# Two transformer blocks on one core: loads of the first stage reordered, a 16-row series cut in three, one weight unit of the scan rounds moved into the chain of steps

## The reference

```
mod = silu(c) @ w_ada + b_ada                    # 12288 numbers for each block
shift_m, scale_m, gate_m, shift_f, scale_f, gate_f = split(mod, 6)
h = rms_norm(x, g) * (1 + scale_m) + shift_m
proj = h @ w_in        ->  q, k, v, xs, z, B, C, dt_raw
dt = softplus(dt_raw + dt_bias)                  # 16 heads x 256 tokens, first block
A_cs = cumsum(dt * -exp(a_log))
x = x + gate_m * mix ;  h = ... ;  x = x + gate_f * conv_ffn(h)
```

## Time and profile before

| what | value |
| --- | --- |
| median of 3 runs | 2723.0 us (2719.33 to 2724.44) |
| the profiled execution, its own time | 2718.6 us |
| its span, first to last instruction | 2716.7 us |
| PE busy | 2491.7 us, 92% of the span |
| DVE busy | 1883.8 us, 69% |
| ACT busy | 1114.1 us, 41% |
| mean granted TensorE clock | 0.951 |
| read from HBM | 607.54 MB |

### The profile page before, as it was taken

One profiled execution on the slowest core, in us unless ns is written; L12 is line 12 of the kernel. 1 busy time (PEld: TensorE's weight loads), 2 busy tenths in 40 slices (PEclk: granted clock), 3 DMA queues, 4 the chain that ended last, 5 costly groups with the idle time before them and its releaser, 6 DMA issues.

```text
span 2716.7 us, 51420 instructions
## 1 busy us (share of the span) xinstructions
PE 2491.7 (92%) x21636; PEld 2411.4 (89%) x21636; DVE 1883.8 (69%) x2215; ACT 1114.1 (41%) x1179; POOL 87.8 (3%) x184
## 2 busy tenths in 40 slices
PE   4889885989999999999979999899899999999997
PEld 4888854989999999999969888789899999999997
DVE  5988768877777677776769766667777654555544
ACT  3234323345554334443343445333555433344433
POOL 0000000000000000000000000000000000000000
PEclk9999966999999999999989999899899999999999
DMA  7987723957776887777938422216576545455442
GB/s 318 392 337 278 283 115 134 367 219 278 278 287 242 332 287 275 277 278 282 329 138 325 159 85 85 99 64 235 213 270 243 184 171 185 170 186 178 177 171 108
DMA packets 87914, 613.56 MB, mean 226 GB/s; under 512 B 9576, under 2 KB 13168, under 8 KB 14320
## 3 DMA queue, kind: packets, MB, share of 16 engines
q1 hardware_dynamic: 64608, 442.95, 44.6%
q0 software_dynamic: 23184, 168.83, 16.1%
HBM read 607.54 MB, written 4.21 MB: 225 GB/s over the span
## 4 chain that ended last, share of the span: by engine, by line
PE 81%; DVE 12%; ACT 3%; issue 2%; DMA 1%; SPq 0%; DVEq 0%; ACTq 0%
PE ps L686 24%; PE ps L688 24%; PE ps L687 24%; DVE first_raw L1484 2%; PE ps L683 2%; DVE w_lo L1472 2%; ACT w_hi L1011 1%; DMA tri<-in_consts 1%; PE ps L573 1%; DVE w_lo L1468 1%; PE ps L818 1%; DVE rstd L1503 1%; PE ps L467 1%; DVE tmp L1511 1%; DVE xbc L1616 1%
## 5 line engine op out<-in xcount | busy, mean ns | idle before, releaser
L686 PE MATMUL ps<-h_hi,w_hi 128*128 128x256 f32 x4480 | 1288.3, 288 | 78.9 <-DVE h_lo L1597 28.3
L688 PE MATMUL ps<-h_hi,w_lo 128*128 128x256 f32 x4480 | 1278.6, 285 | 0.0
L687 PE MATMUL ps<-h_lo,w_hi 128*128 128x256 f32 x4480 | 1278.5, 285 | 0.0
L1468 DVE TENSOR_TENSOR w_lo<-w_raw,w_hi 128x2048 fp32r<-128x2048 f32 x307 | 703.7, 2292 | 534.8 <-ACT w_hi L1006 531.0
L1006 ACT CAST w_hi<-w_raw 128x2048 fp32r<-128x2048 f32 x306 | 583.5, 1907 | 1005.2 <-PE ps L688 972.2
L686 PEld LDWEIGHTS ps<-h_hi,w_hi 128*128 128x128 f32 x4480 | 871.2, 194 | 90.2 <-issue 33.6
L687 PEld LDWEIGHTS ps<-h_lo,w_hi 128*128 128x128 f32 x4480 | 871.6, 195 | 0.4
L688 PEld LDWEIGHTS ps<-h_hi,w_lo 128*128 128x128 f32 x4480 | 870.4, 194 | 0.0
L686 PE MATMUL ps<-hid_hi,w_hi 128*128 (+1 forms) x1408 | 397.3, 282 | 21.8 <-issue 21.8
L687 PE MATMUL ps<-hid_lo,w_hi 128*128 (+1 forms) x1408 | 396.6, 282 | 0.0
L688 PE MATMUL ps<-hid_hi,w_lo 128*128 (+1 forms) x1408 | 396.4, 282 | 0.0
(11 more groups left out here) (331 smaller groups left out, 1531.8 us busy)
## 6 DMA issues: line engine op xcount, KB each, us to landing
w_raw<-in_w_stream SPq DMA_DIRECT2D x376, 1024.0 KB, 4.8
ada_raw<-in_ada_stream POOLq DMA_DIRECT2D x160, 1024.0 KB, 6.8
first_raw<-in_ada_stream SPq DMA_DIRECT2D x32, 1024.0 KB, 7.4
x<-in_x_t SPq DMA_DIRECT2D x1, 2048.0 KB, 13.8
x_kept<-x SPq DMA_DIRECT2D x1, 2048.0 KB, 7.3
out_t<-x SPq DMA_DIRECT2D x4, 512.0 KB, 2.7
ada_c<-in_c SPq DMA_DIRECT2D x1, 1024.0 KB, 4.4
ada_c<-in_c POOLq DMA_DIRECT2D x1, 1024.0 KB, 6.1
```

The costliest lines, as they stand in the source:

```text
L686: mm(o, hi, r_hi, start=first, stop=False, **kw)
L687: mm(o, hi, r_lo, start=False, stop=False, **kw)
L688: return mm(o, lo, r_hi, start=False, stop=last, **kw)
L1468: tt(w_lo[:, slot], w_raw[:, slot], w_hi[:, slot % 2].bitcast(F32), ALU.subtract).then_inc(lo_ready, 1)
```

## The change

1. **Loads and order of the first stage.** SP issues c, ones, x, params, rows 0 to 3, weight unit 0, rows 4 to 7; then for k = 1 to 15 weight unit k followed by rows 2(k + 3) and 2(k + 3) + 1 as long as k + 3 < 16; ident, tri and rel_bias behind all of these. DVE makes eight products ahead of the variance, and products within the loop from k = 4 on. `stat(0)` waits for ones alone; the wait for the other two constants goes to the first transpose that needs them. ACT takes the root ahead of the casts of units 0 and 1.
2. **Softplus in three parts** (5, 8 and 6 statements) behind units (5, 3), (6, 0) and (6, 3). The products of (5, 3) and (6, 3) are taken out, one is put at (6, 2), and five instead of four stand ahead of `var(3)`.
3. **Sixth unit of the rounds**: two of its eight parts behind the `u` product of each of the four steps, in rounds 0, 1 and 3.

```diff
             sp.dma_start(ada_c[:], a["c"].partition_broadcast(P)).then_inc(c_in, 16)
-            sp.dma_start(par[:], a["params"]).then_inc(par_in, 16)
-            load_first_ada(0)
-            load_first_ada(1)
             sp.dma_start(ones[:], a["consts"][:, CCOL["ones"]:CCOL["ones"] + P]).then_inc(con_in, 16)
             sp.dma_start(x[:], a["x_t"]).then_inc(x_in, 16)
-            load_first_ada(2)
-            load_first_ada(3)
+            sp.dma_start(par[:], a["params"]).then_inc(par_in, 16)
+            for q in range(4):
+                load_first_ada(q)
             load_w(U_QK, 0, True)
-            load_w(U_QK + 1, 1, True)
+            for q in range(4, 2 * AHEAD):          # AHEAD = 4
+                load_first_ada(q)
+            for k in range(1, KT):
+                load_w(U_QK + k, k % 4, k < 4)
+                if k + AHEAD - 1 < KT:
+                    load_first_ada(2 * (k + AHEAD - 1))
+                    load_first_ada(2 * (k + AHEAD - 1) + 1)
             sp.dma_start(ident[:], ...)
             sp.dma_start(tri[:], ...)
             sp.dma_start(relb[:], a["rel_bias"]).then_inc(relb_in, 16)
-            for k in range(2, KT):
-                load_first_ada(2 * k)
-                load_first_ada(2 * k + 1)
-                load_w(U_QK + k, k % 4, k < 4)
             units(KT, U_OUT1 + 4)
...
                     last.then_inc(S("u_mm"), 1)
+                if i != 2:
+                    pair(*units[5], ks=(2 * q, 2 * q + 2))
                 if q == 3:
                     break
...
-            if i != 2:
-                pair(*units[5], ks=(0, 2))      # ahead of y_sum
...
-            if i != 2:
-                pair(*units[5], ks=(2, 4))      # behind y_sum
...
-            if i != 2:
-                pair(*units[5], ks=(4, 8))      # behind y_sq_sum
...
-            pe.wait_ge(con_in, 48)
+            pe.wait_ge(con_in, 16)
             stat(0)
...
             pe.wait_ge(S("decays"), 1)
+            pe.wait_ge(con_in, 48)
...
             stat(0, xs, 0)
+            root(0)
             hi_unit(U_QK)
             hi_unit(U_QK + 1)
-            root(0)
...
-            for q in range(4):
+            for q in range(2 * AHEAD):
                 first_ada(q)
             var(0, D)
             inverse(0)
             for k in range(KT):
-                if k >= 2:
+                if k >= AHEAD:
                     first_ada(2 * k)
                     first_ada(2 * k + 1)
...
-            in1_ada = (..., (1, 1, 1, 1), (0, 1, 0, 1), (1, 1, 1, 1))
+            SOFTPLUS = {(5, 3): 0, (6, 0): 1, (6, 3): 2}
+            in1_ada = (..., (1, 1, 1, 0), (0, 1, 1, 0), (1, 1, 1, 1))
...
                     next_ada(in1_ada[c][i])
-                if c == 6:
-                    softplus()
+                    if (c, i) in SOFTPLUS:
+                        softplus(SOFTPLUS[c, i])
...
-            next_ada(4)
+            next_ada(5)
```

More of the change, by code:

```diff
@@ L43 @@
 FFN_A, FFN_B = 12, 10
+AHEAD = 4
 UNIT = 2048
@@ L1629, in in1_evac, with softplus @@
                     V.tensor_copy(v_tok[:, 1, o:o + 512], ps[:, 4 * par_ + 1, :]).then_inc(dve_evac, 1)
-            def softplus():
+            def softplus(part):
                 XV, EV, SV, S2 = (sp_w[:, i] for i in range(4))
                 NA = sp_w[:, 4, 0:1]
[L1635 to L1648, removed]
@@ new lines, in softplus @@
+                if part == 0:
+                    dve.wait_ge(S("dt_exp"), 2)
+                    steps.link(ts(SV, EV, 2.0, None, ALU.add))
+                    steps.link(V.reciprocal(SV, SV))
+                    steps.link(tt(SV, SV, EV, ALU.mult))
+                    steps.link(tt(S2, SV, SV, ALU.mult))
+                    steps.link(ts(EV, S2, 1.0 / 19.0, None, ALU.mult))
+                elif part == 1:
+                    for k in range(8, 0, -1):
+                        steps.link(stt(out=EV, in0=EV, scalar=1.0 / (2 * k + 1), in1=S2, op0=ALU.add, op1=ALU.mult))
+                else:
+                    steps.link(stt(out=EV, in0=EV, scalar=1.0, in1=SV, op0=ALU.add, op1=ALU.mult))
+                    steps.link(ts(XV, XV, 0.0, None, ALU.max))
+                    steps.link(stt(out=dtcs[:, 0], in0=EV, scalar=2.0, in1=XV, op0=ALU.mult, op1=ALU.add))
+                    steps.link(ts(SV, dtcs[:, 0], NA, -1.0, ALU.mult, ALU.mult))
+                    steps.link(V.memset(S2, 1.0))
+                    V.tensor_tensor_scan(dtcs[:, 1], S2, SV, 0.0, ALU.mult, ALU.add).then_inc(S("decays"), 1)
@@ L1656, in next_ada @@
                     pair += 1
-            in1_ada = ((0, 0, 0, 1), (1, 1, 1, 1), (0, 1, 1, 1), (0, 1, 1, 1), (0, 1, 1, 1), (1, 1, 1, 1), (0, 1, 0, 1),
+            SOFTPLUS = {(5, 3): 0, (6, 0): 1, (6, 3): 2}
+            in1_ada = ((0, 0, 0, 1), (1, 1, 1, 1), (0, 1, 1, 1), (0, 1, 1, 1), (0, 1, 1, 1), (1, 1, 1, 0), (0, 1, 1, 0),
                        (1, 1, 1, 1))
```

## The result

| | before | after |
| --- | --- | --- |
| median (runs) | 2721.16 us (4, 2719.03 to 2724.44) | 2803.53 us (4, 2798.23 to 2810.57) |
| ratio, 95% interval | | 1.0303 (1.0275 to 1.0332) |
| profiled execution, span | 2716.7 us | 2798.3 us |
| mean granted clock | 0.951 | 0.940 |

The change costs 82.4 us; the forecast was +84.4 us and 2807 us. Most lines of the kernel after stand three or four lower: L1481 is the product (L1484 before), L1469 the lower part, L1008 the cast and L1594 `h_lo` of the first stage, L682 to L684 PE's three products.

What follows compares the result with a forecast made beforehand. TensorE was busy 92% of the span, with DVE bounding the first stage at 7.87 us a turn. Terms +92.6 - 7.5 + 4.3 - 5.0 = +84.4 us on 2723.0 gave 2807 us, range 2790 to 2832.

Steps and rivals of the forecast that it cites:

- The ring of the first stage: First stage: each weight unit issued behind its own turn's products, a closed chain; ten turns of 17.7 us, +92.6 us.
- t(4): First stage: end of the second DVE product of turn 4, forecast at 65.9 against 72.0 before, 6.1 us ahead.
- the term of issue and landing: First stage: time from a turn's second product until its weight unit has been issued and has landed, taken as 8.7 us.
- either bound: First-stage landing limits: 7.9 us gives 16.9 a turn, +85 (chance 0.13); 10.8 gives 19.8, +114 (0.07).
- The 7.5 us: Softplus: PE's wait for a lower part behind the uncut series, forecast to vanish once cut, -7.5 us.
- The fifth product: Ahead of the attention's var(3): its load goes only once the third product is done, delaying the variance, +4.3 us.
- Rounds 0 and 1 end 2.2 us sooner: Scan rounds: full products in the steps keep the clock at 2.4 GHz, so these two rounds each end 2.2 us sooner.
- Nothing is won by the exchange itself: Rounds' tail: moving the pieces into the steps leaves 16.4 us against 16.3; only the clock changes.
- Round 3 is bound by its tail, and wins 0.6: Last scan round: bound by cast, lower part and add_half(5), so it gains only 0.6 us.
- the rounds lose: Rival, scan rounds: clock stays low in spite of the added parts, +15 us for the three, 2827 us; chance 0.18.
- A weight unit hidden anyway: Rival, first stage: the unit is there when the cast wants it, sum -14.3, 2709 us; chance 0.05.
- A ring that dissolves: Rival, first stage: the block dissolves after a few turns, half the excess, about 2758 us; chance 0.05.

Runs made afterwards that it cites:

- list_two_turns: Changed kernel with SP's weight units 1 to 3 first, then rows 2k, 2k+1 and unit k, waiting on products two turns before; 2711.87 us.
- list_one_turn: Changed kernel with units 1 and 2 first, then rows 2(k+1), 2(k+1)+1 and unit k, waiting on products one turn before; 2719.16 us.
- rounds_first_only: Kernel before with the pieces of the sixth unit in the steps of round 0 alone; 2720.45 us.
- early_softplus_half: Kernel before with x early, four products ahead, three-part softplus with its (6, 3) product kept, half the sixth unit in steps of rounds 0, 1, 3; 2688.41 us.

## Why the prediction was right, point by point

**The ring of the first stage** was right in every link. t(4) was forecast at 65.9 and came at 66.2, the first unit at 43.4 (43.8), the turn at 17.7 (17.43), t(14) at 243.3 (240.5). The +92.6 us measured +89.8 at t(14): only the term of issue and landing was mis-sized, 8.39 us in the mean where I took 8.7 from the two rows of before. It stands nearer to the two rows than to either bound (7.9 and 10.8). list_two_turns shows that the order of the list causes the loss, list_one_turn that it does so as a ring and in the size that a ring gives.

The Trainium skill (DMA: Bandwidth & Descriptors, Anatomy of one DMA) says that waits are done by the issuing sequencer ahead of dispatch. The trace agrees: no weight unit is issued before the products of its turn, and the wait is booked to SP, 173.9 us. Its 2.0 us plus bytes at 436 GB/s is a fit that the section gives for loads issued by GpSimd, while these units are issued by SP, which the prediction did not say. By the prediction's estimate from it the landing would come 7.0 us behind t(k) and a turn take 16.0; 8.39 and 17.43 were measured, so behind two other loads the measurement stands above that sum.

**Part 2.** The 7.5 us went, and a little more. From the qk evacuation to the `dt_tok` copy the six traces without the cut series take 190.1 to 192.3 us, 191.6 in the mean, and the eight with it 181.0 to 183.4, in the mean 181.9: 9.7 us gained. What I left out was what follows a stall: before, PE had lost the full clock behind it (granted 0.50 in the 3 us from 330, 0.77 in the 3 us from 333, 1.00 in the 8 us from 314 and again from 336). That this makes up the other 2.2 us is an argument; no run separates it. The fifth product, forecast at +4.3, cost 4.3 by the trace and 3.8 by the medians.

**Part 3 was wrong in its net**, -5.0 forecast, +2.5 measured. Its first steps held: the clock stayed up (0.98 to 1.00), a step took 3.9 us (forecast 2.47 + 1.44), and round 0 became shorter by 1.9 in the means (forecast 2.2). The steps of the prediction that failed are two. "Rounds 0 and 1 end 2.2 us sooner": round 1 gained 0.4. Behind this stands "Nothing is won by the exchange itself (16.4 against 16.3)", with a tail that "just fits". It did not fit: with the pieces gone from the tail of rounds 0 and 1, PE waits 0.48 us for `y_sum` where it had no wait and 1.47 in place of 0.78 us for the lower part behind `lora_mm`. These two take 1.2 us of each round; what takes the rest is not shown. "Round 3 is bound by its tail, and wins 0.6": it lost 1.6, because what is bound by a tail pays for every matmul put ahead of that tail; the four longer steps delay `add_half(5)`, and PE's wait for it grows from 2.10 to 4.97. The pieces behind `y_sq_sum` had covered that tail. And round 2, of which I said nothing, is 3.4 us longer in the means. Together -1.9 - 0.4 + 3.4 + 1.6 = +2.7, near the +2.5 and +2.7 of the medians.

The split between rounds 2 and 3 is less sure than their sum. Of the seven traces with the rounds as before, the two with a long round 2 (87.9) have a short round 3 (147.5), the five others 84.1 and 150.1 to 150.5 (rounds_first_only, with 84.2 and 147.6, fits neither). Set against those two alone, the whole unit costs 0.7 us in round 2 and 3.6 in round 3, which is nearer to the 2.9 us by which the wait grew. The rival "the rounds lose" had the sign but not the mechanism: it put the loss on a low clock.

The Trainium skill (TensorE: Matmul & The Clock Gate, What's actually happening) holds that activity releases the higher clock. The trace agrees for the steps, 0.61 to 1.00 with either the whole or half of the unit in them. That a full clock in the steps makes the kernel faster whatever stands behind them, the runs with the whole unit do not bear out.

**The other rivals.** A weight unit hidden anyway (2709): it needed another list, and with that list the kernel took 2711.9. A ring that dissolves: ten turns of 17.43 us in a row, none did.

**The total** is near in part by offset. By the trace (+81.7 against +84.4) the ring is 2.7 us less than forecast, part 2 another 2.2 less, the rounds 6.9 more (+1.9 in this trace where I had -5.0), and 4.7 us went in stretches that the diff does not touch (-2.0 from `dt_tok` to `logit`, -2.7 from `var(3)` to round 0). Such shifts are no finding: over all fourteen traces the first of these stretches takes 66.5 to 69.5 us and the second 1048.0 to 1052.3.

Open: why round 2 is 84.1 us in some traces and 87.9 to 89.1 in others, at a granted clock of 0.94 or 0.88 with unchanged code. All five kernels with the whole unit in the steps have the long one, but so have two of the eight traces whose round 1 is unchanged. A depth of more than four slots of `first_raw` was not tried.

## What to carry to other kernels

In a queue that issues in order, write for each load whose work its wait stands for, and how many turns back that is; what stands behind it inherits the wait. If the load behind is needed in the very turn whose products release it, the turn becomes the whole ring, and its price is the ring divided by the turns that it spans. To fill a low-clock stretch with matmuls from elsewhere, take no more than keeps the clock up, and leave the tail behind it its cover: half a unit gained 7.6 us where the whole gained nothing (+2.7, not clear of zero).

## What the runs showed that I had not expected

- A queue's wait costs far more than its bytes: with the same 607.54 MB read in the whole, the DMA share of the first stage fell from 1.00 (64 to 150 us) to 0.51 (66 to 240 us).
- With fewer products ahead the kernel was faster: 2704.9 us with four, 2711.9 with eight, both with the two-turn list (the second has the other two parts of the change too, -5.9 and +2.5).
- The granted clock shifts single stages by some 2 us between two executions of the same program (round 0: 83.37 and 81.49), while rounds 1 and 2 repeat to 0.02.
- The best kernel of the study, early_softplus_half, is 1.2% faster than before: 2688.41 against 2721.12 us.
